# Expert weights of a 32-expert feed-forward stage loaded in 1 MB transfers with 8 KB rows and one semaphore each

## The reference, cut to what matters

```
logits = hf @ router_w + router_b            # 32 experts, top 4, softmax over the four
for e in range(32):
    gu  = hf @ w_gate_up[e] + b_gate_up[e]    # w_gate_up[e]: 1024 x 2048 float32, 8 MB
    g, lin = gu[:, :1024], gu[:, 1024:]       # clamped at 7
    act = g * sigmoid(1.702 g) * (lin + 1)
    out = out + combine[:, e] * (act @ w_down[e] + b_down[e])   # w_down[e]: 1024 x 1024, 4 MB
```

## Time and profile before

| | us |
|---|---|
| median of 3 runs (1171.83 to 1173.54) | 1172.03 |
| profiled execution | 1168.89 |
| its span, first to last instruction | 1167.1 |
| TensorE busy (modelled) | 990.0 |
| VectorE busy | 320.3 |
| ScalarE busy | 131.2 |
| GpSimd busy | 14.9 |
| data moved | 434.87 MB, mean 373 GB/s |
| mean granted TensorE clock | 0.932 |

### The profile page before, as it was taken

How to read it: one execution, slowest core, us unless ns; L and a number is a source line. 1 busy time by engine, 2 the same in 40 slices (tenths; PEclk the granted TensorE clock), 3 DMA queues, 4 the chain that set the end, 5 groups by cost and what they waited for, 6 DMA issues and landing times.

```text
span 1167.1 us, 23860 instructions
## 1 busy us (share of the span) xinstructions
PE 990.0 (85%) x10044; PEld 462.9 (40%) x10045; DVE 320.3 (27%) x949; ACT 131.2 (11%) x292; POOL 14.9 (1%) x26
## 2 busy tenths in 40 slices
PE   8999999999966667689999997699776997977695
PEld 6887886433422222224444332243222342422242
DVE  5999943421211111112212211122111211111112
ACT  2211230500000000000000000000000000000002
POOL 1111000000000000000000000000000000000000
PEclk9999999999998887879999998799878999997898
DMA  9763687695999999997999999999999999999994
GB/s 260 233 169 110 224 331 287 251 424 233 427 427 424 429 424 427 426 427 301 422 411 399 426 426 427 426 425 427 426 425 426 426 426 426 426 426 428 425 426 195
DMA packets 69355, 434.87 MB, mean 373 GB/s; under 512 B 15232, under 2 KB 31552, under 8 KB 36560
## 3 DMA queue, kind: packets, MB, share of 16 engines
q1 hardware_dynamic: 69184, 434.41, 90.9%
q10 hardware_dynamic: 144, 0.09, 0.1%
HBM read 431.69 MB, written 1.05 MB: 371 GB/s over the span
## 4 chain that ended last, share of the span: by engine, by line
PE 45%; DMA 41%; DVE 9%; SPq 3%; issue 2%; ACT 0%; ACTq 0%; DVEq 0%
DMA ring<-in_w_gate_up 24%; PE ps L1478 17%; DMA ring<-in_w_down 13%; PE ps L1491 8%; DMA early<-in_w_gate_up 3%; PE ps L1444 3%; PE ps L1362 2%; PE ps L1413 2%; PE ps L1224 2%; PE ps L1435 2%; PE ps L1467 2%; SPq L369 2%; SPq L366 1%; PE ps L1460 1%; PE ps L1378 1%
## 5 line engine op out<-in xcount | busy, mean ns | idle before, releaser
L1478 PE MATMUL ps<-ring,base 128*32 128x512 f32 x2208 | 294.3, 674 | 115.8 <-DMA ring<-in_w_gate_up 99.4
L1478 PEld LDWEIGHTS ps<-ring,base 128*32 128x32 f32 x2208 | 74.1, 117 | 307.2 <-issue 156.3
L1491 PE MATMUL ps<-ring,base 128*32 128x256 f32 x2944 | 177.5, 381 | 11.5 <-DMA ring<-in_w_down 11.1
L1491 PEld LDWEIGHTS ps<-ring,base 128*32 128x32 f32 x2944 | 89.7, 110 | 101.6 <-issue 33.4
L1131 DVE TENSOR_SCALAR base<-ps 128x256 f32<-128x256 f32 x46 | 19.5, 425 | 379.6 <-PE ps L1478 379.6
L1224 PE MATMUL ps<-ring 128*128 128x256 f32 (+1 forms) x448 | 103.4, 390 | 0.0
L1224 PEld LDWEIGHTS ps<-ring 128*128 128x128 f32 x448 | 84.9, 192 | 15.8 <-issue 1.4
L697 ACT ACTIVATE base<-base 128x256 f32<-128x256 f32 x46 | 19.1, 416 | 628.5 <-DVE base L1131 628.5
L1087 DVE TENSOR_TENSOR base<-ps,base 128x256 f32<-128x256 f32 x47 | 20.0, 425 | 203.3 <-PE ps L1453 203.3
L1478 PE MATMUL ps<-early,base 128*32 128x512 f32 x368 | 52.4, 694 | 16.3 <-DMA early<-in_w_gate_up 16.3
L1478 PE MATMUL ps<-late,base 128*32 128x512 f32 x368 | 50.1, 666 | 13.6 <-DMA late<-in_w_gate_up 13.6
(11 more groups left out here) (323 smaller groups left out, 687.4 us busy)
## 6 DMA issues: line engine op xcount, KB each, us to landing
ring<-in_w_gate_up SPq DMA_DIRECT2D x96, 2048.0 KB, 38.8
ring<-in_w_down SPq DMA_DIRECT2D x63, 2048.0 KB, 40.6
late<-in_w_gate_up SPq DMA_DIRECT2D x16, 2048.0 KB, 40.5
early<-in_w_gate_up SPq DMA_DIRECT2D x16, 2048.0 KB, 39.8
ring<-in_w_in SPq DMA_DIRECT2D x14, 1024.0 KB, 7.8
ring<-in_w_out SPq DMA_DIRECT2D x4, 1024.0 KB, 13.0
ring<-in_w_s_lin SPq DMA_DIRECT2D x2, 1024.0 KB, 6.1
ring<-in_w_s_gate SPq DMA_DIRECT2D x2, 1024.0 KB, 5.4
```

The costliest lines, as they stand in the source:

```text
L1478: ins = nc.tensor.matmul(ps[BS * q:BS * q + BS, 0, :].rearrange("p (a c) -> p a c", a=2), xT[:, k % 2, k // 2, :], row[:, :, QW * q:QW * q ...
L1491: ins = nc.tensor.matmul(ps[BS * q:BS * q + BS, 1, 0:QW], actT[:, n % 2, n // 2, :], row[:, out_cols(q)], start=(n == 0), stop=(n == KT - ...
```

## The change

Every load of expert weights becomes a DMA of 1 MB in which each of the 128 partitions gets one piece of 8 KB. For gate_up this is one row k (successive partitions start 64 KB apart in HBM), for down one quarter q. Each buffer of 1 MB has a semaphore of its own: 8 for gate_up and 4 for down, for even and for odd experts. SP waits for `gu_done` of each row and for `dn_done` of each two groups before it issues the load that overwrites them. TensorE waits for each row in `gate_up`, and for each quarter in `down`. The semaphore `dn_tail`, the NOPs and the special case of the last expert go. The order of the loads, the buffers and the computation stay.

```
-        gu_in = [[sem(f"gu_{name}{n}") for n in range(NPAIR)] for name in ("even", "odd")]
-        dn_in = [[sem(f"dn_{name}{n}") for n in range(2)] for name in ("even", "odd")]
+        gu_in = [[sem(f"gu_{name}{k}") for k in range(KT)] for name in ("even", "odd")]
+        dn_in = [[sem(f"dn_{name}{n}") for n in range(NQ)] for name in ("even", "odd")]
...
             rows = T["w_gate_up"][0, e:e + 1].rearrange("o (p k) n -> p (o k) n", k=KT)
-            return rows[:, PAIR * n:PAIR * n + PAIR, :].rearrange("p k n -> p (k n)")
-        def dn_rows(e, h):
-            return T["w_down"][0, e].rearrange("(q p j) n -> p q (j n)", q=NQ, j=2)[:, 2 * h:2 * h + 2, :]
+            return rows[:, n, :]
+        def dn_rows(e, q):
+            return T["w_down"][0, e].rearrange("(q p j) n -> p q (j n)", q=NQ, j=2)[:, q, :]
...
-            def whole(tail):
-                sp.nop().then_inc(tail, 16)
+            def load_gu_row(e, k):
+                sp.dma_start(gsl[e % 2][k // PAIR][:, (k % PAIR) * SLOT:(k % PAIR) * SLOT + SLOT], gu_rows(e, k)
+                             ).then_inc(gu_in[e % 2][k], 16)
+            def load_dn_row(e, q):
+                sp.dma_start(dsl[e % 2][q // 2][:, (q % 2) * SLOT:(q % 2) * SLOT + SLOT], dn_rows(e, q)
+                             ).then_inc(dn_in[e % 2][q], 16)
             def load_gu(e, n):
-                sp.dma_start(gsl[e % 2][n], gu_rows(e, n)).then_inc(gu_in[e % 2][n], 16)
+                for k in range(PAIR * n, PAIR * n + PAIR):
+                    load_gu_row(e, k)
             def load_dn(e, h):
-                sp.dma_start(dsl[e % 2][h].rearrange("p (q c) -> p q c", q=2), dn_rows(e, h)).then_inc(dn_in[e % 2][h], 16)
+                for q in range(2 * h, 2 * h + 2):
+                    load_dn_row(e, q)
...
             for e in range(2, EXP):
                 before = used_by(e - 2)
-                for n in range(NPAIR):
-                    sp.wait_ge(gu_done, before * KT + PAIR * (n + 1))
-                    load_gu(e, n)
-                if e < EXP - 1:
-                    for h in range(2):
-                        sp.wait_ge(dn_done, before * KT + 4 * (h + 1))
-                        load_dn(e, h)
-                    whole(dn_tail)
-                else:
-                    ...
+                for k in range(KT):
+                    sp.wait_ge(gu_done, before * KT + k + 1)
+                    load_gu_row(e, k)
+                for q in range(NQ):
+                    sp.wait_ge(dn_done, before * KT + 2 * (q + 1))
+                    load_dn_row(e, q)
...
             def gate_up(e, odd, first, until):
                 for k in range(PAIR * first, PAIR * until):
                     n = k // PAIR
-                    if k % PAIR == 0:
-                        pe.wait_ge(gu_in[odd][n], e * 8 + 16 - 8 * odd)
+                    pe.wait_ge(gu_in[odd][k], e * 8 + 16 - 8 * odd)
...
             def down(e, odd, h):
-                pe.wait_ge(dn_in[odd][h], e * 8 + 16 - 8 * odd)
                 for n in range(4 * h, 4 * h + 4):
-                    if n == 6:
-                        pe.wait_ge(dn_tail, e * 16 + 16)
+                    if n % 2 == 0:
+                        pe.wait_ge(dn_in[odd][n // 2], e * 8 + 16 - 8 * odd)
```

More of the change, by code:

```diff
@@ L276, in build @@
         taps_in, conv_dve = sem("taps_in"), sem("conv_dve")
-        scales, dn_tail = sem("scales"), sem("dn_tail")
+        scales = sem("scales")
         rows_in, bc_in, cp_ready = sem("rows_in"), sem("bc_in"), sem("cp_ready")
```

## The result

| | median us | runs | ratio to before, 95% interval |
|---|---|---|---|
| before | 1172.03 | 5 (1171.83 to 1173.54) | |
| changed | 1178.93 | 5 (1175.19 to 1180.09) | 1.0050 (1.0032 to 1.0068) |
| changed, again | 1177.86 | 5 (1177.20 to 1179.47) | 1.0048 (1.0035 to 1.0061) |

So the change makes the kernel about half a per cent slower, 5.8 to 6.9 us by the medians. The forecast was +3.2 us, about half of that. The range held the result only at its very end (1178.93 against 1179); the part that the forecast had given to itself, 1173 to 1177.5 us, did not.

The account below looks back on a forecast made before the run. The weight stream and TensorE were taken to bound the kernel in turns. For the profiled execution 1168.89 + 6.8 - 3.6 = 1172.1 us; against the median 1172.03 + 3.2 = 1175.2 us, 0.27% slower, range 1171.5 to 1179.

Parts of the forecast that it names:

- two stream-bound stretches: From 278 to 517 us and 615 to 1110 us TensorE waits for the weight stream; forecast 2.2 and 4.6 us longer.
- The price of the stream: Gate_up in 8 KB pieces costs 0.068 us more for 2 MB, 0.27 us an expert, +6.8 us in all.
- The hand-overs: Where the bound passes between stream and TensorE, finer waits let work start earlier at four places: -3.6 us together.
- SP's two: At the DMA idle stretches ending near 279 and 615 us, SP is released one row earlier: -0.86 us each.
- TensorE's two: At 517.14 and 1110.17 us, only two groups of down remain after the last quarter lands: -0.96 us each.
- rival A: No change to be seen: TensorE's hand-overs pay the whole half-clock row, 1.46 us at both; 1174.2 us, chance 0.22.
- What costs nothing: SP's 12 issues an expert in place of 6, TensorE's five more waits, the NOPs and dn_tail: counted as no time.
- B: Faster: the 8 KB price belongs to down's two-piece transfer, not piece size, so no stream term; 1168.4 us, chance 0.10.
- C: Slower by more: each DMA carries a cost of its own; 1186 us, at worst some 345 us more; chance 0.08.
- bound of +18 us: Upper bound of the stream's term, taking literally the 2.52 us between the last two 1 MB landings, over 25 experts.
- TensorE's five added waits: Four in gate_up, one in down, counted as nothing; bound 4.6 us over some 12 blocks, a third in the range.

Follow-up runs that it names:

- before_again: The kernel before the change, run once more unchanged for its spread and a second trace: 1172.42 us, ratio 1.0002.
- after_again: The changed kernel, run once more unchanged for its spread and a second trace: 1177.86 us, ratio 1.0048.
- Tensor_waits_coarse: The changed kernel, but TensorE waits for two rows of gate_up or two quarters of down at a time: 1179.53 us, ratio 1.0068.
- dn_quarters: The kernel before, with only down loaded in 1 MB quarters, each with its own semaphore and waits: 1172.49 us, ratio 0.9997.
- gu_2mb_8kb: The kernel before, with each 2 MB gate_up DMA written as two adjoining 8 KB rows for a partition: 1171.34 us, ratio 1.0004.
- gu_partition_halves: The kernel before, with each gate_up pair loaded in two 1 MB DMAs of 64 partitions each, in 16 KB pieces: 1952.84 us.
- gu_2mb_rows_apart: The kernel before, with each 2 MB gate_up DMA made of rows n and n + 4, so really in 8 KB pieces: 1180.17 us, ratio 1.0069.
- down_16kb_time_only: The kernel before, with down in 16 KB pieces and gate_up's columns left, so its sums differ: 1167.58 us, ratio 0.9967.
- gu_rows_pair_waits: The kernel before, with gate_up loaded in 1 MB rows but still released and awaited by pairs: 1179.07 us, ratio 1.0066.

## Why the prediction was right in kind and half in size

The two second traces, before_again and after_again, both have the long half-clock stretch at 223 us, so they can be compared leg by leg. Times are spans of TensorE's or SP's timeline in us:

| leg | before | changed | measured | forecast |
|---|---|---|---|---|
| start to SP's first issue after the first idle stretch | 281.56 | 280.89 | -0.67 | -0.86 |
| from there to expert 10's last part of down taken up | 238.91 | 241.19 | +2.28 | +2.2 |
| from there to the next block | 2.37 | 1.95 | -0.42 | -0.96 |
| from there to SP's issue after the last idle stretch | 95.20 | 94.45 | -0.75 | -0.86 |
| from there to expert 30's last part of gate_up taken up | 495.57 | 500.88 | +5.31 | +4.6 |
| from there to the next block | 12.55 | 12.13 | -0.42 | -0.96 |
| two blocks, to the last scatter | 33.42 | 33.37 | -0.05 | 0 |
| last scatter to the end | 11.2 | 11.9 | +0.7 | 0 |
| sum | 1170.8 | 1176.8 | +6.0 | +3.2 |

(The hand-over at 517.14 is at 520.47 in this trace of before, and at 522.08 in the changed kernel's; the rows stand below.)

- **Which legs count** was right: the two stream-bound stretches lose, the four places of hand-over gain, and of the rest only the last scatter moves (+0.7).
- **The price of the stream**, +6.8 us: mechanism right, size a little low (this is 0.8 us of the 2.8 that the forecast missed). Measured 7.6 us. An expert takes 29.83 us and not 29.80, as a row of 1 MB comes every 2.487 us, between the 2.483 of down's halves and the 2.52 of the two last transfers. The page of the Trainium skill that was weighed, DMA: Bandwidth & Descriptors, section "Measured (HBM→SBUF, 128 partitions, SWDGE, issued from GpSimd)", with 6.15 us for 1 MB, was as far off as the trace of before had said: 2.487 us were measured, with 10 transfers and more in flight (26.3 us from issue to landing). The 341 GB/s of the same row would have given 3.1 us, an estimate from that page which the prediction did not make, and is too slow as well.
- **The hand-overs**, -3.6 us: this is the step that failed in size; measured -2.3, 1.3 us of what was missed. SP's two came out nearly whole (-0.67 and -0.75 of -0.86). TensorE's two gave 0.42 each and not 0.96. What I had not counted is the sequencer work between two blocks. Before, the last wait that holds TensorE up stands ahead of a block's last four groups, 1.93 us of matmuls, and the sequencer works towards the next block beside them. With the held-up wait ahead of the last two groups only about half of that is left to hide it, and the gap before the next block grows. Before_again, then after_again, TensorE's timeline:

```profile
520.47 1.93 PE L1491 MATMUL ps<-ring,base 128*32 128x256 f32 x32 [1.67 <-DMA ring<-in_w_down]
522.84 7.07 PE L1478 MATMUL ps<-ring,base 128*32 128x512 f32 x64 [0.43 <-issue]
...
1126.16 7.30 PE L1478 MATMUL ps<-ring,base 128*32 128x512 f32 x64 [0.67 <-issue]
```

```profile
522.08 1.07 PE L1484 MATMUL ps<-ring,base 128*32 128x256 f32 x16 [1.19 <-DMA ring<-in_w_down]
524.03 6.22 PE L1472 MATMUL ps<-ring,base 128*32 128x512 f32 x56 [0.88 <-issue]
...
1129.30 1.07 PE L1484 MATMUL ps<-ring,base 128*32 128x256 f32 x16 [0.97 <-DMA ring<-in_w_down]
1131.49 7.21 PE L1472 MATMUL ps<-ring,base 128*32 128x512 f32 x64 [1.12 <-issue]
```

  The gap goes from 0.43 to 0.88 us at the first hand-over and from 0.67 to 1.12 at the last, 0.45 us each, of the 0.54 that are missing at each. Tensor_waits_coarse puts the wait back ahead of the four groups and leaves the transfers as they are: its gaps are 0.52 and 0.70 us. So the place of the wait makes the gap; that it is the sequencer's work which fills it is argued.
- **Clock**: I had priced the half clock only as rival A, and as a gain. The kernels in which TensorE waits row by row have mean clocks of 0.908 to 0.921 in all their runs, before and those that wait by pairs 0.923 to 0.946 (lowest in dn_quarters), but for one run of gu_2mb_8kb at 0.895 and for gu_partition_halves. Most of that lies where TensorE waits for the stream anyway. At the end it falls on the last scatter (1.92 and 2.09 us in the two traces of the changed kernel, 1.15 in both of before) and gives the +0.7 us. But kernels in which gate_up waits by pairs had 2.09 there too (gu_2mb_8kb, dn_quarters), so how much of this is chance stays open.
- **What costs nothing**: SP's doubled issues and TensorE's finer waits held. Six blocks take 93.33 us in place of 93.22, 0.02 us a block. The issue's latency fell to 26 us without a trace of it.
- **Rivals.** A is out: TensorE's hand-overs gave 0.42 us each and not 1.46. B is out: the pieces cost, whatever the transfer is. C is out as a cost of the transfer (dn_quarters, gu_2mb_rows_apart), and its bound of +18 us with it; that the result is slower than the forecast, as C has it, has other reasons.
- **Luck in the range.** Its last 1.5 us, up to 1179, were kept for TensorE's five added waits, which cost 0.02 us a block. What brought the time up there were the gap behind the moved wait, the stream's 0.8 us and the last scatter. So the range held for a reason that it didn't name, by 0.07 us in the first series and 1.1 in the second.

## What to carry to other kernels

When a queue is kept full, price a load by its contiguous pieces, not by its transfers: here 8.5 to 9.5 ns for each piece on an engine, 0.3 us for 8 MB when 16 KB becomes 8 KB, whether the DMA has 1 or 2 MB. Finer transfers pay only at the few places where the bound passes between the stream and an engine, so list these places first, count what the finer wait gains there, and look at what the sequencer still has to do behind the last wait. And compare no two single traces by their ends: a stretch at half clock in one of them was worth 3.7 us here, more than the 3.2 us that were forecast for the change.

## What the runs showed of the hardware that was not expected

- A transfer over 64 partitions ran at about 216 GB/s with all DMA engines busy, one over 128 at 426; cutting a pair by partitions made the kernel 1.5 to 1.7 times as long (1794.10 to 2012.97 us). The Trainium skill has the rule, SBUF — State Buffer, section "Door 1: The DMA port swizzle": bandwidth goes with how many of SBUF's ports the partitions of a transfer reach, and either half of the 128 reaches half of them. The trace agrees: 216 is half of 426. Two transfers over the two halves, issued one after the other, don't make up for it here: the rate stays at about 216 GB/s as long as gate_up is loaded.
- A DMA written with two rows for a partition that lie together goes as one piece (69355 packets, as before).
- The queue's depth follows neither transfers nor bytes: 38.8 us at 4.9 us each is 7.9 transfers of 2 MB before, 26.3 us at 2.49 is 10.6 of 1 MB after. Counted in pieces of one engine it is about 85 both times (before has 64 pieces in six transfers), but this doesn't hold further: 32.2 us in gu_2mb_rows_apart are 104 pieces, 38.6 us in down_16kb_time_only 63. What the queue counts stays open.
- Waits that stand in pairs one after the other cost TensorE 0.1 to 0.2 us a block (six blocks take 93.85 us in gu_rows_pair_waits, with four such pairs a block, 94.43 in tensor_waits_coarse, with six, and 93.22 before), the same waits spread over the rows and quarters 0.02.
